# Mixer scores as rounded products of stacked query parts, 30-column products spread between weight products, and keys turned inside the next unit

## The reference, cut to what matters

```python
proj = x @ w_in[l]                       # [256, 2560 + 24]
(h_a, b_a, c_a, uv, q, kc, vc, ksl, vsl, kw, vw, gl) = jnp.split(proj, split_points, axis=-1)
y_a = short_conv(h_a, b_a, c_a, conv_w[l])
y_b = gmlp_spatial(uv, gmlp_ln_g[l], gmlp_ln_b[l], gmlp_w[l], gmlp_b[l])
y_c = nsa_attention(q, kc, vc, ksl, vsl, kw, vw, gl, ...)
mix = jnp.concatenate([y_a, y_b, y_c], axis=-1) @ w_out[l]
x = layer_norm_2(ALPHA * x + mix, ln2_g[l], ln2_b[l])
```

## Time and profile before

| | before |
|---|---|
| median of 3 runs | 1907.75 us (1907.04 to 1908.02) |
| the profiled execution | 1906.78 us, its span 1905.0 us |
| mean granted clock of PE | 0.986 |
| PE, matmuls: busy, share, instructions | 1860.3 us, 98%, 9118 |
| PE, weight loads | 1549.1 us, 81% |
| DVE | 1295.7 us, 68% |
| ACT | 1006.0 us, 53% |
| POOL | 123.5 us, 6% |
| moved by DMA | 426.56 MB, mean 224 GB/s |

### The profile page before, as it was taken

How to read it: one execution, slowest core, us unless ns; L and a number is a source line. 1 busy time by engine, 2 the same in 40 slices (tenths; PEclk the granted TensorE clock), 3 DMA queues, 4 the chain that set the end, 5 groups by cost and what they waited for, 6 DMA issues and landing times.

```text
span 1905.0 us, 21839 instructions
## 1 busy us (share of the span) xinstructions
PE 1860.3 (98%) x9118; PEld 1549.1 (81%) x9118; DVE 1295.7 (68%) x1313; ACT 1006.0 (53%) x1069; POOL 123.5 (6%) x105
## 2 busy tenths in 40 slices
PE   7999999998999999998999999999999999999998
PEld 6788888887978888886888887888888888778886
DVE  4569999997778898997555657655464545676544
ACT  6446777774646777774443364444344424635431
POOL 1021000001011000000000300100010003020000
PEclk9999999999999999998999999999999998999999
DMA  9447999996435999996555642655565556336551
GB/s 339 152 147 249 358 370 359 357 361 201 145 129 196 370 356 358 357 372 213 179 196 172 214 138 88 202 194 169 188 221 178 177 175 206 120 131 201 184 178 59
DMA packets 220170, 426.56 MB, mean 224 GB/s; under 512 B 7560, under 2 KB 28304, under 8 KB 220064
## 3 DMA queue, kind: packets, MB, share of 16 engines
q1 hardware_dynamic: 214256, 406.91, 62.0%
q0 software_dynamic: 5808, 18.17, 3.0%
HBM read 423.99 MB, written 1.06 MB: 223 GB/s over the span
## 4 chain that ended last, share of the span: by engine, by line
PE 92%; DVE 4%; ACT 2%; DMA 1%; issue 1%; POOL 0%; DVEq 0%; SPq 0%
PE ps L447 26%; PE ps L449 26%; PE ps L448 26%; DVE Wlo L416 2%; PE ps L558 2%; PE ps L2429 1%; PE ps L2399 1%; PE ps L2335 1%; ACT Whi L404 1%; PE ps L1544 1%; PE ps L538 1%; PE ps L537 1%; PE ps L536 1%; PE ps L2415 1%; PE ps L1937 1%
## 5 line engine op out<-in xcount | busy, mean ns | idle before, releaser
L416 DVE TENSOR_TENSOR Wlo<-raw,Whi 128x2048 fp32r<-128x2048 f32 (+2 forms) x387 | 868.3, 2247 | 445.1 <-ACT Whi L404 444.4
L404 ACT ACTIVATE Whi<-raw 128x2048 fp32r<-128x2048 f32 (+2 forms) x393 | 736.3, 1877 | 480.6 <-PE ps L449 476.1
L447 PE MATMUL ps<-Whi,XTh 128*128 128x512 f32 (+2 forms) x1504 | 579.3, 385 | 14.2 <-DVE Wlo L416 8.1
L449 PE MATMUL ps<-Whi,XTl 128*128 128x512 f32 (+2 forms) x1504 | 569.7, 379 | 0.0
L448 PE MATMUL ps<-Wlo,XTh 128*128 128x512 f32 (+2 forms) x1504 | 569.4, 379 | 0.0
L447 PEld LDWEIGHTS ps<-Whi,XTh 128*128 128x128 f32 x1504 | 287.6, 191 | 70.7 <-DVE Wlo L416 9.6
L449 PEld LDWEIGHTS ps<-Whi,XTl 128*128 128x128 f32 x1504 | 286.8, 191 | 52.5
L448 PEld LDWEIGHTS ps<-Wlo,XTh 128*128 128x128 f32 x1504 | 287.4, 191 | 49.8 <-issue 0.5
L447 PE MATMUL ps<-Whi,hTh 128*128 128x512 f32 x352 | 137.7, 391 | 0.0
L449 PE MATMUL ps<-Whi,hTl 128*128 128x512 f32 x352 | 137.1, 389 | 0.0
L448 PE MATMUL ps<-Wlo,hTh 128*128 128x512 f32 x352 | 137.0, 389 | 0.0
(11 more groups left out here) (327 smaller groups left out, 1867.5 us busy)
## 6 DMA issues: line engine op xcount, KB each, us to landing
raw<-in_moe_w_gate SPq DMA_DIRECT2D x64, 1024.0 KB, 5.4
raw<-in_moe_w_up SPq DMA_DIRECT2D x64, 1024.0 KB, 5.5
raw<-in_moe_w_down SPq DMA_DIRECT2D x64, 1024.0 KB, 5.7
raw<-in_ffn_gate SPq DMA_DIRECT2D x44, 1024.0 KB, 5.1
raw<-in_ffn_up SPq DMA_DIRECT2D x44, 1024.0 KB, 5.1
raw<-in_ffn_down SPq DMA_DIRECT2D x40, 1024.0 KB, 5.0
raw<-in_w_in SPq DMA_DIRECT2D x18, 1024.0 KB, 6.4
raw<-in_a_w_in SPq DMA_DIRECT2D x10, 1024.0 KB, 12.3
```

Source lines behind the costliest of these rows:

```text
L404: act.activation(Whi[:, i % NS, 0:m * n], raw[:, i % NR, 0:m * n], ACT.Copy).then_inc(w_rounded, tick(w_rounded, "rounded", i))
L416: dve.tensor_tensor(Wlo[:, i % NR, 0:m * n], raw[:, i % NR, 0:m * n], h.bitcast(f32), ALU.subtract).then_inc(w_rest, tick(w_rest, "rest", i))
L447: pe.matmul(o, xh(k, t), h[:, q, :], start=k == first, stop=False)
L449: x = pe.matmul(o, xl(k, t), h[:, q, :], start=False, stop=k == end)
```

## The change

- **Scores.** The float32 query copy `qT` and the padded keys `kz` go. `qs` holds for each group the rounded queries (fp32r) in the group's 64 partitions and their remainders in the other 64; `kh` holds the rounded keys in both halves, `kl` their remainders. One head's scores are `qs` by `kh` over 128 rows plus high queries by `kl` over 64 rows, both fp32r. ACT makes the rounded copies, DVE the remainders. The compressed keys `kc` hold both parts side by side, so the two columns of a score are added by a reduction on DVE.
- **30-column products.** `hidden_cmp(i)` is handed to `use_unit` as `each` and places its 16 products between the weight products: i=0 in the second unit of q, t=1, i=1 in the first unit of kw, t=0.
- **Windows, keys.** `windows` and `k_turn` are now hooks (`second`) within the first unit of q and of uv. `gmlp` moves from after the scores of item 3 to before `turn_(5)`.

```diff
+            if each:
+                each(3 * q)
             pe.matmul(o, xh(k, t), l[:, q, :], start=False, stop=False)
+            if each:
+                each(3 * q + 1)
+                if q < m - 1:
+                    each(3 * q + 2)
             x = pe.matmul(o, xl(k, t), h[:, q, :], start=False, stop=k == end)
...
+        def hidden_cmp(i):
+
+            def some(n):
+                if n == 0:
+                    bank(pe, "hg", l, i)
+                    pe.wait_ge(*on("kpe", l))
+                    pe.wait_ge(*on("mx", l))
+                b = where["hg", l, i]
+                for lh in range(16 * n // 11, 16 * (n + 1) // 11):
                     x = pe.matmul(PS[b][:, 0:30], M.w1[i][:, lh, :], M.kpe[:, i, lh].rearrange("p g n -> p (g n)"),
                                   start=lh == 0, stop=lh == 15)
...
-                    x = pe.matmul(PS[b][:, 128 * t + 32 * r:128 * t + 32 * r + 32], qT[:, r, t * 128:(t + 1) * 128],
-                                  M.kcz[:, :, :].rearrange("p g n -> p (g n)"), start=True, stop=True)
+                    for g in range(2):
+                        c = 256 * t + 64 * r + 32 * g
+                        x = pe.matmul(PS[b][:, c:c + 32], M.qs[:, g, r, t * 128:(t + 1) * 128],
+                                      M.kc[:, g].rearrange("p n a -> p (n a)"), start=True, stop=True)
...
-                    pe.matmul(s[:, 2 * j:2 * j + 2, :], qT[:, r, t * 128:(t + 1) * 128], kz[:, g, :, 0:kn],
-                              start=j == 0, stop=False)
+                    c = slice(t * 128, t * 128 + 128)
+                    pe.matmul(s[:, 2 * j:2 * j + 2, :], M.qs[:, g, r, c], M.kh[:, g, :, 0:kn], start=j == 0, stop=False)
+                    pe.matmul(s[:, 2 * j:2 * j + 2, :], M.qs[ps, g, r, c], M.kl[ps, :, 0:kn], start=False, stop=False)
...
-        for z in run("q"):
-            if z == 0:
-                windows()
-            if z == 1:
-                hidden_cmp()
-        for z in run("kw"):
+        for z in run("q", second=windows, each={(1, 1): hidden_cmp(0)}):
+            pass
+        for z in run("kw", each={(0, 0): hidden_cmp(1)}):
...
-        k_turn()
-        for z in run("uv"):
+        for z in run("uv", second=k_turn):
...
+        gmlp()
         turn_(5)
...
+            for i in range(2):
+                act.wait_ge(*on("qT", l, i))
+                for g in range(2):
+                    ps = slice(64 * g, 64 * g + 64)
+                    act.activation(M.qs[ps, g, 2 * i:2 * i + 2, :],
+                                   PS[where[("qT", l, i)]][ps, :].rearrange("p (h n) -> p h n", n=256),
+                                   ACT.Copy).then_inc(act_done, tick(act_done, "qTs", l, i, g))
...
+            for g in range(2):
+                ps, to = slice(64 * g, 64 * g + 64), slice(64 - 64 * g, 128 - 64 * g)
+                act.wait_ge(*on("kTo", l, g))
+                act.activation(M.kh[to, g], M.kh[ps, g].bitcast(f32), ACT.Copy).then_inc(
+                    act_done, tick(act_done, "kTs", l))
...
+                    dve.wait_ge(*on("qTs", l, i, g))
+                    dve.tensor_tensor(M.qs[to, g, c, :], PS[where[("qT", l, i)]][ps, :].rearrange("p (h n) -> p h n", n=256),
+                                      M.qs[ps, g, c, :].bitcast(f32), ALU.subtract).then_inc(
+                        dve_done, tick(dve_done, "qTl", l, i))
...
+        def k_turn():
+            for g in range(2):
+                ps = slice(64 * g, 64 * g + 64)
+                dve.wait_ge(*on("kTo", l, g))
+                dve.tensor_tensor(M.kl[ps], PS[where[("kT", l)]][ps, :].rearrange("p (h n) -> p h n", n=256),
+                                  M.kh[ps, g].bitcast(f32), ALU.subtract).then_inc(dve_done, tick(dve_done, "kTl", l))
```

More of the change, by code:

```diff
@@ L434, in load_units, with use_unit @@
                 w_landed[i % NR], tick(w_landed[i % NR], "landed", i, by=16))
-    def use_unit(pe, i, t, b, xh, xl, ready, first, end, at=None, what=None):
+    def use_unit(pe, i, t, b, xh, xl, ready, first, end, at=None, what=None, each=None):
         _, m, n, k0, _ = units[i]
@@ L451, in use_unit, with job_pe @@
         point[("prod", i, t)] = point[("used", i)]
-    def job_pe(pe, name, xh, xl, ready, nt=2, skew=False, hold=0, second=None, turn=None):
+    def job_pe(pe, name, xh, xl, ready, nt=2, skew=False, hold=0, second=None, turn=None, each=None):
         bs = [bank(pe, name, t, hold=True) for t in range(nt)]
@@ L465, in job_pe @@
                     here = second and z == 0 and t == 0 and i == group[-1]
-                    use_unit(pe, i, t, bs[t], xh, xl, ready, 0, nk - 1, 3 * units[i][1] // 4 if here else None, second)
+                    use_unit(pe, i, t, bs[t], xh, xl, ready, 0, nk - 1, 3 * units[i][1] // 4 if here else None, second,
+                             each[z, t] if each and (z, t) in each else None)
             if group[-1] == last:
@@ L2327, in windows @@
                     x.then_inc(pe_done, tick(pe_done, "window", l, i, g))
[L2329 to L2334, removed]
+        def hidden_cmp(i):
[6 more added lines that the diff above has]
+                for lh in range(16 * n // 11, 16 * (n + 1) // 11):
                     x = pe.matmul(PS[b][:, 0:30], M.w1[i][:, lh, :], M.kpe[:, i, lh].rearrange("p g n -> p (g n)"),
                                   start=lh == 0, stop=lh == 15)
-                x.then_inc(pe_done, tick(pe_done, "hg", l, i))
+                if n == 10:
+                    x.then_inc(pe_done, tick(pe_done, "hg", l, i))
+            return some
         def q_turn():
@@ L2502, in mixer_pe @@
                 turn_(3)
-                gmlp()
         for z in run("cb"):
@@ L2537, in evac_q, with hidden_cmp, hidden_rows @@
             free(act_done, ("mx", l, "q"), t)
-        def hidden_cmp():
-            for i in range(2):
-                act.wait_ge(*on("zeros", l))
-                act.wait_ge(*on("mx", l))
-                act.wait_ge(*on("hg", l, i))
-                act.activation(M.hg[:, i, :, 0:15], PS[where[("hg", l, i)]][:, 0:30].rearrange("p (g n) -> p g n", g=2),
-                               ACT.Gelu_apprx_tanh,
-                               bias=b1[:, i:i + 1]).then_inc(act_done, tick(act_done, "hgs", l, i))
-                free(act_done, "hg", l, i)
+        def hidden_cmp(i):
+            act.wait_ge(*on("zeros", l))
+            act.wait_ge(*on("mx", l))
+            act.wait_ge(*on("hg", l, i))
+            act.activation(M.hg[:, i, :, 0:15], PS[where[("hg", l, i)]][:, 0:30].rearrange("p (g n) -> p g n", g=2),
+                           ACT.Gelu_apprx_tanh,
+                           bias=b1[:, i:i + 1]).then_inc(act_done, tick(act_done, "hgs", l, i))
+            free(act_done, "hg", l, i)
+        def hidden_rows():
             act.wait_ge(*own(act_done))
```

76 lines of the change are left out of this document (42 added, 34 removed).

## The result

| | before | changed |
|---|---|---|
| median time | 1907.88 us (1907.04 to 1908.42, 4 runs) | 1920.43 us (1919.69 to 1920.68, 4 runs) |
| profiled execution, its span | 1906.78, 1905.0 us | 1919.69, 1917.9 us |
| mean granted clock of PE | 0.986 | 0.985 |

A forecast was written before the change was run, and what follows sets the result against it. The prediction saw TensorE, busy 98% of the span, as the bound. Its terms, 9.4 + 8.3 - 6.2 + 1.6 - 3.0 + 1.6, gave 11.7 us gained: 1895.1 us profiled, 1896.1 median, range 1890 to 1902.

The forecast's parts named there:

- Scores, +9.4: Scores in both mixers: two rounded products replace each float32 one, 6.4 us won at t=1 heads, 3.0 at t=0 banks.
- Rows count for nothing: Score products: row count does not change the price, since a 16-row product takes 613 ns and a 128-row one 599.
- Rival C: Score pairs: weight loads are not hidden, 7.4 us less gain, 1903.5 us; chance 0.06.
- 30-column products, +8.3: q and kw: interleaved among weight products they keep the clock up, 10.08 us per layer at full clock; 8.3 us won.
- rival A: Mixers: the clock falls at a new place, giving 1899.5, 1902.9 or 1904.4 us; chance 0.2.
- Windows, -6.2: Window transposes moved into q's first unit wait for DVE's `twice`: 3.1 us lost per layer, 6.2 in all.
- Keys, +1.6: Key transposes moved into uv's first unit: a shorter wait for ACT wins 1.6 us in two layers.
- the wait shrinks from 1.28 to about 0.5: Key transposes: PE arrives at 6.75 us after the query transposes, kw's last copy ends at about 7.2.
- ACT would be later by some 1.1 us: kw's last copy out of PSUM ends about 7.2 us after the query transposes instead of 6.1.
- First flips, -3.0: First flips: their second half waits for the bank ACT empties late, 1.5 us lost per layer, 3.0 in all.
- gmlp, +1.6: Gated block's 16 records, moved between flips and values of item 3, fill the 0.78 us wait: 1.6 us won.
- Rival D: Mixers: the windows' wait drops the clock, the thin mix keeps it down until kw's 280-column stream, 1930.7 us; chance 0.04.

The follow-up runs named there:

- e1: The changed kernel with the second product of each score pair over all 128 rows, the other 64 rows zero: 1911.5 us.
- e8: The kernel before with only the scores' part of the change, second products over 128 rows, order of work as before: 1901.9 us.
- e2: The changed kernel with the PSUM bank of uv's second half taken only when that half begins: 1919.0 us.
- e11: The kernel before with only the gated block's products moved behind the last flips: 1904.7 us.
- e3: The changed kernel with the window transposes back behind all 24 products of q's first unit: 1927.6 us.
- e6: The kernel before with only the interleaving of the 30-column products, window transposes left where they were: 1921.3 us.
- e14: e12 with the 30-column products starting 1.36 us earlier in q, over 33 places, one for each: 1902.3 us.
- e10: e12 with the 30-column products back in the changed kernel's 22 places: 1908.2 us.
- e9: e12 with both products of a score pair over the same 64 rows, queries' remainders times rounded keys left out: 1898.0 us.
- e12: The change plus edits of e1, e2, e3, 30-column products later in 27 places, compressed values' product in uv, uv's banks held until the first flips: 1890.1 us.

## Why the prediction was wrong

It was 24 us off and on the wrong side. Two things make up the 24.6 us between the forecast and the profiled executions: 12.8 in the scores and 11.9 in the clock. What the other terms were off by nearly cancels. By its own steps:

- *Scores, +9.4.* Measured -3.4: nothing at the t=1 heads, 8 x 0.4 lost at the t=0 banks. **The step that failed is "Rows count for nothing".** It compared the mean durations of a 16-row and a 128-row product. The prediction itself says that durations say little and starts count, and neither row shows a change from one kind to the other. What the runs showed in its place: 0.20 us for each change between 64 and 128 rows, 12.8 us in all, and the clock falling behind the first scores besides (6.8 us of loss in the change, none in e1). Every other price of this term was right, as e1 and e8 show. Rival C (7.4 us less gain, given without its working) had over half of this loss for another reason. Weight loads of the same rows are hidden, at 0.23 and 0.12 us from start to start in e1; the trace disagrees with the rule of the Trainium skill that C leaned on (TensorE: Matmul & The Clock Gate, Part 3: Packing small matmuls). The same section of the Trainium skill also lets a load into the background weight buffer go ahead of matmuls in flight. That would allow what the trace shows; which buffer a load takes no run here shows.
- *30-column products, +8.3.* In their own stretch they brought 6.1: the clock held there in both mixers of the profiled execution, 0.62 us in each layer went to a bank, and the mix took 10.55 us where 10.08 was priced (from 1093.26 to the query transposes at 1106.93, less 11 products of 512 columns and the 0.62). But the term took the lost clock as this stretch's own and asked only of this stretch whether it would hold. In the mixers 8.5 us of loss became 11.9, all of it elsewhere: 6.8 behind the first scores, 3.4 behind uv's wait, 1.7 behind the windows' wait. That is rival A, with 0.2 and at most 8.3 us. And the 1.00 in the stretch itself was luck: e1 and e2, whose products are the same up to there, lost 5.1 us in three of four mixers.
- *Windows, -6.2.* Right: 2.61 us in each layer, -5.2.
- *Keys, +1.6.* Measured -2.1. The step "the wait shrinks from 1.28 to about 0.5" followed the data to the transposes and not the banks to the unit ahead of them. With the transposes behind uv's start, uv's first product is what asks first for the bank that ACT frees last: 2.35 us in place of 1.28. That ACT would be later by some 1.1 us was right (1.0).
- *First flips, -3.0.* Not there, since PE comes 2 us late; in e1 it is (1.72), in e8 too (1.3).
- *gmlp, +1.6.* Right or better (2.5 in e11).
- *Clock in the mixers.* -3.4 (8.5 us lost before, 11.9 now); this holds what the 30-column stretch won back too.

The measured parts are the scores -3.4, the clock -3.4, the bank in kw -1.2, the mix -0.9, the windows -5.2, the keys -2.1 and gmlp +1.6: -14.6, against -12.9 between the two profiled executions. The 1.7 us between them I can't place.

Rival D (a wait drops the clock and a thin mix keeps it down) had 0.04 and was placed at the windows. There it happened in the second layer only and was brief. Behind the wait for the mixer's weights it is what e3, e6 and e14 show. What decides in one execution whether such a wait ends in a loss of 3 or of 14 us is open (1.54 us in e10 ended in 3.4, 1.09 in e3 in 10.2): the edits here could only take the waits away, and not steer the fall behind one.

## What to carry to other kernels

When an edit gives a matmul fewer rows than its neighbours, count the changes of kind between consecutive matmuls and not the rows: here zeros in the unused half cost PE nothing and saved 12.8 us of its time. When a transpose or product moves past the start of a unit, write down the bank rotation for both orders and who frees each bank last. And a gain that rests on a clock that will hold is booked in full only when no wait stands ahead of the stretch and several executions show 1.00 in it; one profiled execution can be luck. Compare kernels by span times granted clock first, and by time over many executions second.

## What was unexpected of the hardware

- Changing from 128-row to 64-row products and back costs 0.38 to 0.40 us, 0.20 a change, whether one, two or four 64-row products of 256 or 512 columns lie between (the change, e9).
- Executions of one kernel differ by up to 23 us (e14), nearly all of it through the granted clock: their full-clock times lie within 1868 and 1873. In e10, 1895.8 us of span at 0.988 and 1917.9 at 0.976 are 1873 and 1872 us at full clock.
- A late start does not make sure of the weights: e12 and e9 are alike up to the scores, and PE waits 0 us for them in one profiled execution and 1.92 in the other.
- The mixer's own weights, whose last load was issued at 1082.45 us in e14, were waited for until 1093.6, 11.2 us later; in the kernel before the median of this load was 9.1.
